# Turning the gated products of a SwiGLU by a DMA transpose instead of by TensorE, in a two-layer transformer trunk

## The reference, cut to what matters

```python
def swiglu(x, w_gate_up, w_down):          # x (256, 1024), w_gate_up (1024, 2*2816), w_down (2816, 1024)
    gate, up = jnp.split(x @ w_gate_up, 2, axis=-1)
    return (jax.nn.silu(gate) * up) @ w_down

h = swiglu(rms_norm(x, g[2]), w_gate_up[layer], w_down[layer])
x = x + rms_norm(h, g[3])
```

## Time and profile before

| | |
|---|---|
| time, median of 3 runs | 766.65 us (766.53 to 766.77) |
| span of the profiled execution, first to last instruction | 765.1 us |
| own time of the profiled execution | not listed apart from the three runs; the span lies 1.55 us under their median |
| granted TensorE clock, mean over the span | 0.997 of full speed |
| PE busy | 756.2 us, 99% |
| ACT busy | 418.7 us, 55% |
| DVE busy | 493.7 us, 65% |
| DMA, mean | 182 GB/s, 139.62 MB |

### The profile page before, as it was taken

One profiled execution on the slowest core, in us unless ns is written; L12 is line 12 of the kernel. 1 busy time (PEld: TensorE's weight loads), 2 busy tenths in 40 slices (PEclk: granted clock), 3 DMA queues, 4 the chain that ended last, 5 costly groups with the idle time before them and its releaser, 6 DMA issues.

```text
span 765.1 us, 13561 instructions
## 1 busy us (share of the span) xinstructions
PE 756.2 (99%) x4731; PEld 651.5 (85%) x4731; DVE 493.7 (65%) x678; ACT 418.7 (55%) x633; POOL 172.6 (23%) x298
## 2 busy tenths in 40 slices
PE   9999999999999999999999999999999999999996
PEld 7999978888888888999899898898888888888884
DVE  5888987675455555777766667668547745544543
ACT  4766667453343343866875867767755444333421
POOL 1000001640000000236655765657302000000000
PEclk9999999999999999999999999999999999999998
DMA  8735675796654554559686786786744755566402
GB/s 246 211 117 153 209 230 165 232 272 201 209 193 164 176 194 123 162 158 236 158 217 157 180 215 167 164 224 204 202 138 147 267 196 188 172 215 209 171 1 55
DMA packets 160452, 139.62 MB, mean 182 GB/s; under 512 B 8217, under 2 KB 149121, under 8 KB 160417
## 3 DMA queue, kind: packets, MB, share of 16 engines
q1 hardware_dynamic: 153344, 131.45, 55.3%
q0 software_dynamic: 6784, 7.41, 5.4%
q10 hardware_dynamic: 288, 0.30, 0.2%
HBM read 138.02 MB, written 1.11 MB: 182 GB/s over the span
## 4 chain that ended last, share of the span: by engine, by line
PE 97%; DMA 1%; issue 1%; SPq 0%; POOL 0%; DVE 0%; DVEq 0%; POOLq 0%; ACT 0%
PE ps L1197 21%; PE ps L1199 20%; PE ps L1198 20%; PE ps L1447 10%; PE ps L1449 5%; PE ps L1203 3%; PE ps L1205 3%; PE ps L1204 3%; PE ps L1361 1%; PE ps L1510 1%; PE ps L1274 1%; PE ps L1291 1%; PE ps L1276 1%; PE ps L1277 1%; PE ps L1249 1%; PE ps L1475 1%
## 5 line engine op out<-in xcount | busy, mean ns | idle before, releaser
L805 DVE TENSOR_TENSOR w_lo<-raw,w_hi 128x2048 fp32r<-128x2048 f32 (+2 forms) x144 | 279.0, 1955 | 41.1 <-ACT w_hi L515 38.8
L515 ACT ACTIVATE w_hi<-raw 128x2048 fp32r<-128x2048 f32 (+2 forms) x144 | 232.8, 1637 | 57.1 <-DMA raw<-in_w_kv_b 25.7
L1197 PE MATMUL ps<-w_hi,xt 128*128 128x512 f32 x352 | 139.6, 396 | 0.0
L1199 PE MATMUL ps<-w_hi,xt 128*128 128x512 f32 x352 | 137.2, 390 | 0.0
L1198 PE MATMUL ps<-w_lo,xt 128*128 128x512 f32 x352 | 136.9, 389 | 0.0
L684 ACT ACTIVATE work<-ps,stat 128x256 f32<-128x256 f32 x44 | 21.0, 477 | 194.7 <-PE ps L1199 194.7
L425 POOL TENSOR_SCALAR stat<-stat 128x1 f32<-128x1 f32 x15 | 8.5, 566 | 443.6 <-ACT work L531 419.6
L1197 PE MATMUL ps<-w_hi,ot 128*128 128x512 f32 x240 | 94.8, 395 | 0.0
L1198 PE MATMUL ps<-w_lo,ot 128*128 128x512 f32 x240 | 93.5, 390 | 0.0
L1199 PE MATMUL ps<-w_hi,ot 128*128 128x512 f32 x240 | 93.5, 390 | 0.0
L1199 PEld LDWEIGHTS ps<-w_hi,xt 128*128 128x128 f32 x352 | 66.1, 188 | 14.1
(11 more groups left out here) (149 smaller groups left out, 1274.9 us busy)
## 6 DMA issues: line engine op xcount, KB each, us to landing
raw<-in_w_gate_up SPq DMA_DIRECT2D x88, 512.0 KB, 4.7
raw<-in_w_kv_b SPq DMA_DIRECT2D x96, 256.0 KB, 4.1
raw<-in_w_down SPq DMA_DIRECT2D x22, 1024.0 KB, 4.8
raw<-in_w_q_b SPq DMA_DIRECT2D x48, 256.0 KB, 4.2
raw<-in_w_qkv_a SPq DMA_DIRECT2D x23, 512.0 KB, 4.8
raw<-in_w_o_a SPq DMA_DIRECT2D x4, 1024.0 KB, 6.5
work<-bias_rows POOLq DMA_DIRECT2D x128, 32.0 KB, 3.6
raw<-in_w_o_b SPq DMA_DIRECT2D x4, 1024.0 KB, 5.1
```

Of the source, the lines that this page charges most:

```text
L515: act.activation(w_hi[:, s % CUT, 0:size(s)], raw[:, s % RAW, 0:size(s)], ACT.Copy).then_inc(hi_made, 1)
L805: dve.tensor_tensor(w_lo[:, c, 0:n], raw[:, s % RAW, 0:n], w_hi[:, c, 0:n].bitcast(F32), ALU.subtract).then_inc(lo_made, 1)
L1197: mm(out, xs[0], ws[0], start=start, stop=False)
L1199: return mm(out, xs[1], ws[0], start=False, stop=stop)
```

## The change

For steps 0 to 9 of each layer, PE no longer transposes. DVE copies each token tile's `hid` into two planes, one of the low and one of the high 16-bit halves of the floats (`part_planes`, 512 halves for each token tile). When both tiles are there, ACT issues one DMA transpose of the 128 x 1,024 halves, SBUF to SBUF (`turn_planes`), and DVE joins the turned halves into floats again (`join_planes`, 1,024 halves) before `cut_hidden`, which now reads SBUF and not PSUM. Step 10 of each layer still goes by PE. In ACT's order the wait for the planes (`planes_ready`) and the issue stand around the third hi of the step; in step 0 right behind the second silu. The planes lie in `delta`, the joined floats in `squares`, both of which the steps did not use before. `gated` loses its wait for PE's transpose; `cut_hidden` gets a wait for the `down` before the last (`w_used`), whose operands it writes over.

```diff
+        hid_words = hid_flat.bitcast(U16).rearrange("p (t n w) -> p t w n", t=NT, w=2)
+        plane_cols = delta[:, 0:NT * FC].bitcast(U16)
+        planes = plane_cols.rearrange("p (w t n) -> p t w n", w=2, t=NT)
+        turned_planes = delta[:, NT * FC:2 * NT * FC].bitcast(U16)
+        joined_flat = squares[:, 0:NT * FC]
+        joined_words = joined_flat.bitcast(U16).rearrange("p (n w) -> p w n", w=2)
...
+            def planes_ready(l, i, j):
+                act.wait_ge(planes_made, j * 4 + 2 * (l * (STEPS - 1) + i) + 2)
+            def turn_planes():
+                act.dma_start_transpose(turned_planes.rearrange("p (b n) -> p b n", n=P), plane_cols
+                                        ).then_inc(planes_turned, 16)
             def swiglu_step(l, s0, i, j, units):        # ACT
                 s = s0 + 3 * i - 1
                 for n, u in enumerate(units):
                     if n < NT and i == 1:
                         silu_of(l, s, i, j, n)
+                    if n == NT and i < STEPS - 1:
+                        planes_ready(l, i, j)
                     hi(u, j)
                     if n < NT and i > 1:
                         silu_of(l, s, i, j, n)
+                if i < STEPS - 1:
+                    turn_planes()
             def swiglu(l, s0, last_units):              # ACT
...
+                planes_ready(l, 0, 0)
+                turn_planes()
                 swiglu_step(l, s0, 1, 0, range(s0 + 5, s0 + 8))
...
             def gated(l, i, j, t):
                 dve.wait_ge(silu_made, j * 4 + 2 * n + t + 1)
-                if i >= 1:
-                    dve.wait_ge(ht_done, j * 2 + n)
+                if l and not i:
+                    dve.wait_ge(ht_done, l)
...
+            def part_planes(l, i, j, t):
+                dve.wait_ge(hid_made, j * 4 + 2 * (l * STEPS + i) + t + 1)
+                dve.tensor_copy(planes[:, t], hid_words[:, t]).then_inc(planes_made, 1)
+            def join_planes(l, i, j):
+                d = l * (STEPS - 1) + i
+                dve.wait_ge(planes_turned, j * 32 + 16 * (d + 1))
+                dve.tensor_copy(joined_words, turned_planes.rearrange("p (w n) -> p w n", w=2)).then_inc(planes_joined, 1)
+                dve.wait_ge(planes_joined, j * 2 + d + 1)
...
-            def cut_hidden(l, i, j):
+            def cut_hidden(l, i, j, s0=None):
+                if i < STEPS - 1:
+                    join_planes(l, i, j)
+                    dve.wait_ge(w_used, j * 6 + s0 + 3 * i + 2)
+                    src = joined
+                else:
+                    dve.wait_ge(ht_done, l + 1)
+                    src = two(6).rearrange("p f (t n) -> p t f n", t=NT)
...
-            def swiglu_step(l, i, j, units):            # DVE
+            def swiglu_step(l, s0, i, j, units):
                 if i > 1:
                     lo(units[0], j)
-                cut_hidden(l, i - 1, j)
+                cut_hidden(l, i - 1, j, s0)
                 gated(l, i, j, 0)
+                if i < STEPS - 1:
+                    part_planes(l, i, j, 0)
                 if i == 1:
                     lo(units[0])
                 if len(units) > 1:
                     lo(units[1], j)
                 gated(l, i, j, 1)
+                if i < STEPS - 1:
+                    part_planes(l, i, j, 1)
...
             def swiglu_step(l, s0, i, j):               # PE
                 s = s0 + 3 * i - 1
                 up(l, s, i, j, 0)
-                transpose_hidden(l, i - 1, j)
                 up(l, s, i, j, 1)
                 down(l, s + 2, i - 1, j)
```

More of the change, by code:

```diff
@@ L103, in build @@
           square, mask, select, out):
-    F32, F32R, BF16 = mybir.dt.float32, mybir.dt.float32r, mybir.dt.bfloat16
+    F32, F32R, BF16, U16 = mybir.dt.float32, mybir.dt.float32r, mybir.dt.bfloat16, mybir.dt.uint16
     ACT, ALU = mybir.ActivationFunctionType, mybir.AluOpType
@@ L184, in build @@
         silu = carve(NT * FC).rearrange("p (t n) -> p t n", t=NT)
-        hid = carve(NT * FC).rearrange("p (t n) -> p t n", t=NT)
+        hid_flat = carve(NT * FC)
+        hid = hid_flat.rearrange("p (t n) -> p t n", t=NT)
+        hid_words = hid_flat.bitcast(U16).rearrange("p (t n w) -> p t w n", t=NT, w=2)
[4 more added lines that the diff above has]
+        joined_words = joined_flat.bitcast(U16).rearrange("p (n w) -> p w n", w=2)
+        joined = joined_flat.rearrange("p (t f n) -> p t f n", t=NT, f=2)
         qb = carve(NG * SEQ, 0).rearrange("p (g n) -> p g n", g=NG)
@@ L265, in build @@
             "up0_done", "silu_made", "hid_made", "ht_done", "ht_hi", "ht_made"))
+        planes_made, planes_turned, planes_joined = (sem(n) for n in (
+            "planes_made", "planes_turned", "planes_joined"))
         block = ctx.enter_context(nc.Block())
@@ L1040, in gated @@
                 dve.wait_ge(silu_made, j * 4 + 2 * n + t + 1)
-                if i >= 1:
-                    dve.wait_ge(ht_done, j * 2 + n)
+                if l and not i:
+                    dve.wait_ge(ht_done, l)
                 dve.scalar_tensor_tensor(hid[:, t, :], bank(4 + t, FC, FC), x_rs(2 * l + 1, t), silu[:, t, :],
                                          ALU.mult, ALU.mult).then_inc(hid_made, 1)
-            def cut_hidden(l, i, j):
-                n, k = l * STEPS + i, hidden_at(i)
-                src = two(6)
-                dve.wait_ge(ht_done, j * 2 + n + 1)
-                dve.tensor_copy(ot[:, 0, k, :], src).then_inc(ht_hi, 1)
+            def part_planes(l, i, j, t):
+                dve.wait_ge(hid_made, j * 4 + 2 * (l * STEPS + i) + t + 1)
+                dve.tensor_copy(planes[:, t], hid_words[:, t]).then_inc(planes_made, 1)
@@ new lines, in join_planes @@
+            def join_planes(l, i, j):
[4 more added lines that the diff above has]
+            def cut_hidden(l, i, j, s0=None):
+                n, k = l * STEPS + i, hidden_at(i)
+                hi_, lo_ = (ot[:, h, k, :].rearrange("p f (t n) -> p t f n", t=NT) for h in range(2))
+                if i < STEPS - 1:
[5 more added lines that the diff above has]
+                    src = two(6).rearrange("p f (t n) -> p t f n", t=NT)
+                dve.tensor_copy(hi_, src).then_inc(ht_hi, 1)
@@ L1051, in cut_hidden @@
                 dve.wait_ge(ht_hi, j * 2 + n + 1)
-                dve.tensor_tensor(ot[:, 1, k, :], src, ot[:, 0, k, :].bitcast(F32), ALU.subtract
-                                  ).then_inc(ht_made, 1)
-            def swiglu_step(l, i, j, units):
+                dve.tensor_tensor(lo_, src, hi_.bitcast(F32), ALU.subtract).then_inc(ht_made, 1)
+            def swiglu_step(l, s0, i, j, units):
                 if i > 1:
                     lo(units[0], j)
-                cut_hidden(l, i - 1, j)
+                cut_hidden(l, i - 1, j, s0)
@@ L1069, in swiglu @@
                 gated(l, 0, 0, 0)
+                part_planes(l, 0, 0, 0)
                 lo(s0 + 3)
                 gated(l, 0, 0, 1)
+                part_planes(l, 0, 0, 1)
                 lo(s0 + 4)
-                swiglu_step(l, 1, 0, range(s0 + 5, s0 + 8))
+                swiglu_step(l, s0, 1, 0, range(s0 + 5, s0 + 8))
                 with dve.Fori(0, (STEPS - 3) // 2) as j:
                     for i in (2, 3):
-                        swiglu_step(l, i, j, range(s0 + 3 * i + 2, s0 + 3 * i + 5))
-                swiglu_step(l, STEPS - 1, 0, last_units)
+                        swiglu_step(l, s0, i, j, range(s0 + 3 * i + 2, s0 + 3 * i + 5))
+                swiglu_step(l, s0, STEPS - 1, 0, last_units)
             dve.memset(rows[:, :], 0.0).then_inc(zeros_made, 1)
@@ L1352, in up, with transpose_hidden @@
                     inst.then_inc(up0_done, 1)
[L1354 to L1358, removed]
+            def transpose_hidden(l):
+                pe.wait_ge(hid_made, 2 * (l * STEPS + STEPS))
+                if l:
+                    pe.wait_ge(ht_made, l * STEPS)
                 for f in range(2):
@@ L1386, in last_steps @@
                 up(l, s, last, 0, 0)
-                transpose_hidden(l, last - 1, 0)
                 up(l, s, last, 0, 1)
                 down_part(l, s + 2, last - 1, 0, 0, FH[:2])
-                transpose_hidden(l, last, 0)
+                transpose_hidden(l)
                 down_part(l, s + 2, last - 1, 0, 0, FH[2:])
```

## The result

The changed kernel takes 779.55 us (778.7 to 780.66, 4 runs) against 766.63 before: 1.0169 times, interval 1.0154 to 1.0183, or 12.9 us slower. Forecast were 760.4 us and a range to 778.0.

A forecast was written before the change was run, and what follows sets the result against it. PE, busy 99% of the span, was taken as the bound: 8.9 us of transposes off, 2.7 us lost to late transfers in steps 0 and 1, so 766.65 - 6.2 = 760.4 us; 8-in-10 range 757.4 to 778.

The forecast's parts named there:

- 20 x 0.45 = 8.9 us off PE: PE, steps 0 to 9 of two layers: 20 groups of four transposes go, each costing PE 0.45 us.
- the copies: DVE in each step: parting 0.5, 0.5 and joining 0.9 us; 2 us more, covered by its idle time.
- the budgets of all steps but 0: Issue to landing without PE waiting: 4.7 us (layer 0) and 6.1 (layer 1) in step 1, 10.4 in steady steps.
- The budget of 5.3 us in step 0 of both layers: Step 0, from the transfer's issue to its landing: at most 5.3 us before down is late, in either layer.
- late landing in steps 0 and 1: Rival: transfer lands 2 us or more after a plain one, PE waits; 771.2 us at 3 us more; chance 0.23.
- The sum through step 1: Lateness carried from step 0 into step 1's down: 1.5 us in layer 0, nothing in layer 1.
- I take the plain transfers as the nearest rows: L = 6.5 in step 0 of both layers: Transfer's time from issue to landing: 6.5 us in step 0, 5.0 and 4.5 in step 1, like plain transfers.
- The block by block rival: Transfer's eight 128x128 blocks run one by one; at 1.3 us each 778.7 us, or 829; chance 0.20 with engines as bound.
- The engines as the bound: Rival, every step: DMA engines' time passes 16.34 us, at 9.3 us a transfer 805 us; chance 0.20 with the block rival.
- both rows that bounded it: DMA engine time of a transfer: 44 ns a packet, 2.8 us of all 16 engines, to 97 ns, 6.2 us.
- The rule that these transposes are as fast as ordinary DMAs: Skill's statement on the transfer, at some 90% of DMA bandwidth; by it the sum would be 757.7 to 760.4.

The follow-up runs named there:

- experiment 1: Changed kernel with parts and joins kept but no DMA transpose issued or awaited, so down gets products not turned: 757.5 us, ratio 0.9879 to the kernel before.
- experiment 7: Changed kernel with 48 (layer 0) and 28 (layer 1) matmuls into an unused bank ahead of the first down: 774.94 us, ratio 1.0113 to before.
- experiment 9: Changed kernel with weights of step 2 and later held for step 0's transfer and GpSimd's DMAs for step 1's: 762.94 us, ratio 0.9951 to before.
- experiment 6: Changed kernel with GpSimd's gains put behind two heads' bias rows in layer 0, behind step 0's transfer in layer 1: 769.86 us, ratio 1.0039 to before.
- experiment 4: Changed kernel with GpSimd's DMAs starting only when step 0's transfer has landed, weights left: 763.97 us, ratio 0.9957 to before.
- experiment 5: Changed kernel with weights of step 2 and later held until step 0's transfer has landed, GpSimd left: 767.4 us, ratio 1.0002 to before.
- experiment 2: Changed kernel with step 0 of each layer transposed by PE again, steps 1 to 9 by DMA: 761.77 us, ratio 0.9939 to before.

## Why the prediction was wrong

**Right: what is removed.** "20 x 0.45 = 8.9 us off PE": 9.3 us by the ratio of experiment 1, with an interval of 8.0 to 10.5. Steps of 16.32 us against 16.34 forecast.

**Right: the copies.** Parting, joining, rounding and subtraction took 0.43, 0.75 to 0.86, 0.43 and 0.69 us against 0.5, 0.9, 0.55 and 0.69, on idle time of DVE. ACT's issue takes 1.25 to 1.4 us, not 0.4, and costs nothing either. The issue also goes out when the third hi starts, not when it ends (the prediction put it at 203.2, where 201.3 would have fitted), so the budgets of all steps but 0 were 1.9 us larger than forecast. ACT in a steady step of the changed kernel:
```profile
213.35 1.92 ACT L525 ACTIVATE w_hi<-raw 128x2048 fp32r<-128x2048 f32 x1 [1.17 <-DVE work L1074]
213.36 1.26 ACTq L703 DMA_TRANSPOSE work<-work  x1
```

**Right: where it is tight.** The budget of 5.3 us in step 0 of both layers gives 16.4 - 5.3 = 11.1 and 12.1 - 5.3 = 6.8 us of waiting; 11.05 and 6.61 were measured. Steady steps hid landings of 3.2 to 6.1 us. The rival of which this is the mechanism, late landing in steps 0 and 1, was named and priced at 3 us more than a plain transfer. The sum through step 1, of which the prediction took the larger, came out too high: with the measured landings it gives 10.1 + 1.0 + 9.0 - 4.7 = 15.4 us in layer 0 and 7.1 + 7.9 - 6.1 = 8.9 in layer 1, and the loss followed step 0 alone, 11.05 and 6.61. In layer 0 the issue in step 1 left at 165.75, 3.4 us before the 169.2 of this sum: 1.9 of them are the third hi, and the 1 us of a later weight did not show.

**Wrong: the step "I take the plain transfers as the nearest rows: L = 6.5 in step 0 of both layers".** L measured 16.4 and 12.1 in step 0, while the 512 KB loads beside it took 7.3 and 6.1 us, and 9.0 and 7.9 in step 1 against 5.0 and 4.5. Weights alone make it 6.8, GpSimd alone 4.6, both together 16.4, where nothing beside it gives 3.1, so the two do not add up. The nearest row was also not the slowest one of the stretch: in the kernel before, the 1 MB load that went out at 142.5 us, about when the transfer does now, landed only after 11.1 us (issues between 137 and 152 us), and after 8.7 in layer 1:
```profile
raw<-in_w_down SPq DMA_DIRECT2D x1, 1024.0 KB, 11.1
```
With 11.1 and 8.7 for L in step 0 the same sum has 9.5 us lost against 8.9 won: no gain, though not yet the measured loss. Put right in the sum, step 0's L alone costs 11.4 us in layer 0 (through step 1, 10.1 + 1.0 + 5.0 - 4.7, just above the 11.1 of step 0) and 6.8 in layer 1: 18.2 lost against 8.9 won, 9.3 us slower, 775.9.

**Missing: the clock.** The sum let PE resume at full speed after a wait. It resumed at 1.2 GHz for some 13 matmuls, 2.8 us a layer; experiment 7 gave back 4.6 of 5.5 us. With it the sum is 781.4, the measured 779.55.

**The block by block rival** came within 1 us of the measured time by chance. With nothing beside it all eight blocks land in 3.1 us, and 20 transfers have a median of 4.0, so a block does not cost 1.3 us. The 1309 ns of the Trainium skill (VectorE: DVE Perf Modes, The three transpose paths) are not per block here. **The engines as the bound** falls too: queue 10 shows 5.0% x 778.9 x 16 / 21,408 = 29 ns a packet, 1.9 us of all 16 engines a transfer, under both rows that bounded it, and steady steps stayed at 16.32 us.

The rule that these transposes are as fast as ordinary DMAs (the Trainium skill, Advanced Engine Details and Errata, X-Bar Transpose (TRN2)) agrees in steady steps, 4.0 us against 4.1 for the plain loads of the same 256 KB (`in_w_kv_b` on the page of the changed kernel), and not in step 0, 16.4 against 7.3 for 512 KB. Nor does it hold for the bandwidth that the prediction quotes with it: alone the transfer moved up to 219 GB/s with the engines 90% busy or more (experiment 9), where plain loads before reached 300 to 437 GB/s in many slices between 137 and 152 us.

**What stays open:** why weights and GpSimd's DMAs together delay the transfer so much more than either. One run of experiment 6 has 15.3 us beside the bias rows, small packets from 12 issues; in layer 1 one load of gains goes with 12.1 and 11.6 us, against 6.8 and 9.6 without it. How the 16 engines share their time between three queues, one of which transposes, was not resolved by any run, and the spread of 6.8 to 9.6 us for equal traffic says that it is not a fixed price.

## What to carry to other kernels

A transfer that replaces engine work must be given a budget stage by stage: here the 16 of steps 2 to 9 had about twice the time that they took or more, and the two at the layers' starts, with weights and GpSimd's DMAs in flight beside them, cost more than all 20 could win. Look at the slowest transfer of the stretch too, not only at the median of the most frequent one. Leaving those steps on the engine pays best: step 0 by PE turned 12.9 us lost into 5 won, steps 0 and 1 by PE, or step 0 by PE and GpSimd's DMAs put off, into some 8. Putting GpSimd's DMAs behind step 0's transfer alone won 2.9, since they then met step 1's; with GpSimd behind step 1's transfer and 1 MB of weights held it was 7. When PE is made to wait for several us, add the slower matmuls behind the wait to the price.

## What the runs showed of the hardware that was not expected

- A DMA transpose of 256 KB inside SBUF landed in 3.1 us alone, in 4.6 beside GpSimd's DMAs, in 6.8 to 9.6 beside 3 MB of weight loads, and in 16.4 beside both. Plain loads in the same stretch went from 7.1 to 7.3 us (512 KB, layer 0), while the 1 MB load issued behind the transpose took 13.9 us, where it took 11.1 in the kernel before and 7.1 in experiment 4.
- After 10.9 us idle PE ran 13 matmuls at the lower clock. Shorter waits were followed by it too: after 3.36 us idle (experiment 4), 3.34 (experiment 5) and 3.92 (experiment 6, layer 1) the matmuls started 0.43 us apart. After 2.82 us idle (experiment 2) they started 0.23 us apart, and the granted clock was 1.00 in that stretch.
- A strided copy of 512 halves takes 0.43 us on VectorE and one of 1,024 halves 0.75 us, less than the 0.69 us of the 512-wide subtraction and the 1.22 us of 1,024 floats.
